# Gated attention in pairs of heads on the two halves of TensorE's array, with the high halves of its result on ScalarE

## What is computed

```python
def gqa_attention(q, k, v):
    B, S, _, HD = q.shape
    G = ATT_HEADS // ATT_KV_HEADS
    nb = S // Q_BLOCK
    qb = q.reshape(B, nb, Q_BLOCK, ATT_KV_HEADS, G, HD).transpose(1, 0, 2, 3, 4, 5)
    scale = HD ** -0.5

    def block(q_blk):
        s = jnp.einsum('bqhgd,bkhd->bhgqk', q_blk, k, preferred_element_type=jnp.float32) * scale
        p = jax.nn.softmax(s, axis=-1).astype(v.dtype)
        return jnp.einsum('bhgqk,bkhd->bqhgd', p, v)
...
        y_att = gqa_attention(q, k, v) @ w_att_out[l]
        y_sgu = spatial_gating(jax.nn.gelu(su), jax.nn.gelu(sv), w_s[l], b_s[l],
                               sgu_ln_g[l], sgu_ln_b[l]) @ w_sgu_out[l]
        merged = jax.nn.sigmoid(ga) * y_att + jax.nn.sigmoid(gb) * y_sgu
        x = x + merged @ w_out[l]
```

## Time and profile before

| | before |
|---|---|
| median of 3 runs (lowest, highest) | 1493.07 us (1492.53, 1499.2) |
| the profiled execution | 1499.87 us |
| its span | 1498.0 us |
| TensorE busy | 1385.2 us (92%) |
| VectorE, ScalarE, GpSimd busy | 616.9, 454.1, 426.5 us |
| mean granted clock of TensorE | 0.975 |
| gated attention, first score to the next stage's first product | 129.41 to 151.84 us |
| chain that ended last | TensorE 66%, DMA 12%, VectorE 10%, GpSimd 5% |

### The profile page before, as it was taken

One profiled execution on the slowest core, in us unless ns is written; L12 is line 12 of the kernel. 1 busy time (PEld: TensorE's weight loads), 2 busy tenths in 40 slices (PEclk: granted clock), 3 DMA queues, 4 the chain that ended last, 5 costly groups with the idle time before them and its releaser, 6 DMA issues.

```text
span 1498.0 us, 22670 instructions
## 1 busy us (share of the span) xinstructions
PE 1385.2 (92%) x8222; PEld 862.5 (58%) x8223; DVE 616.9 (41%) x1323; ACT 454.1 (30%) x786; POOL 426.5 (28%) x197
## 2 busy tenths in 40 slices
PE   7999988899999989997899999899998979999985
PEld 6886776544444488775344444498876844444432
DVE  5598444522122243446233333477015254333324
ACT  4554433212121245543111111245435321112101
POOL 6892743100000077051000000279845610000000
PEclk9999999999999999999999999999998989999998
DMA  7664567699999974419699999795525499999951
GB/s 282 221 191 170 184 225 280 276 426 428 428 429 429 410 282 175 170 57 384 248 384 425 430 428 427 276 342 178 204 78 225 138 376 425 385 427 427 428 202 54
DMA packets 89597, 447.62 MB, mean 299 GB/s; under 512 B 7804, under 2 KB 9768, under 8 KB 70952
## 3 DMA queue, kind: packets, MB, share of 16 engines
q1 hardware_dynamic: 85856, 445.87, 74.8%
q10 hardware_dynamic: 3656, 0.57, 0.3%
HBM read 445.38 MB, written 1.05 MB: 298 GB/s over the span
## 4 chain that ended last, share of the span: by engine, by line
PE 66%; DMA 12%; DVE 10%; POOL 5%; issue 3%; ACT 3%; SPq 0%; DVEq 0%; ACTq 0%; POOLq 0%
PE ps L415 62%; DMA ring_hi<-in_w_up 9%; POOL WLO L2383 4%; PE ps L828 1%; PE ps L868 1%; DMA ring_lo<-in_w_co 1%; ACT WHI L1257 1%; PE ps L849 1%; DVE Z L1846 1%; DVE Z L1834 1%; DVE Z L1847 1%; DVE Z L1845 1%; DMA ring_lo<-in_w_ckv 1%; POOL RS L2352 1%; DMA ring_lo<-in_w_out 1%
## 5 line engine op out<-in xcount | busy, mean ns | idle before, releaser
L2383 POOL TENSOR_TENSOR WLO<-ring_lo,WHI 128x1024 fp32r<-128x1024 f32 (+1 forms) x158 | 386.8, 2470 | 686.5 <-ACT WHI L1257 684.7
L415 PE MATMUL ps<-ring_hi,Z 128*64 128x512 f32 x1248 | 280.1, 598 | 8.1 <-DVE Z L2082 3.0
L415 PE MATMUL ps<-ring_lo,Z 128*64 128x512 f32 x1152 | 261.4, 603 | 6.3 <-issue 5.2
L1257 ACT ACTIVATE WHI<-ring_lo 128x1024 fp32r<-128x1024 f32 (+1 forms) x160 | 165.3, 1048 | 217.5 <-PE ps L415 179.7
L415 PEld LDWEIGHTS ps<-ring_hi,Z 128*64 128x64 f32 x1248 | 90.1, 137 | 175.1 <-issue 168.7
L415 PEld LDWEIGHTS ps<-ring_lo,Z 128*64 128x64 f32 x1152 | 83.1, 139 | 159.6 <-issue 159.1
L2085 DVE TENSOR_TENSOR Z<-ps,Z 64x512 f32<-64x512 f32 x50 | 34.7, 694 | 305.1 <-ACT Z L1446 303.3
L415 PE MATMUL ps<-WHI,HTH 128*128 128x512 f32 x320 | 126.9, 397 | 8.9 <-POOL WLO L2383 5.0
L2352 POOL TENSOR_TENSOR RS<-MS,NEGH 128x1 f32<-128x1 f32 (+2 forms) x26 | 22.3, 857 | 370.2 <-DVE MS L1683 309.7
L1446 ACT ACTIVATE Z<-ps 64x512 f32<-64x512 f32 x50 | 29.5, 590 | 322.1 <-PE ps L415 322.1
L415 PE MATMUL ps<-WHI,HTL 128*128 128x512 f32 x320 | 125.2, 391 | 0.0
(11 more groups left out here) (293 smaller groups left out, 1950.3 us busy)
## 6 DMA issues: line engine op xcount, KB each, us to landing
ring_lo<-in_ada_w SPq DMA_DIRECT2D x22, 2048.0 KB, 9.1
ring_lo<-in_moe_w_gate SPq DMA_DIRECT2D x16, 2048.0 KB, 10.3
ring_lo<-in_moe_w_up SPq DMA_DIRECT2D x16, 2048.0 KB, 14.7
ring_lo<-in_moe_w_down SPq DMA_DIRECT2D x16, 2048.0 KB, 13.8
ring_hi<-in_moe_w_gate SPq DMA_DIRECT2D x16, 2048.0 KB, 11.0
ring_hi<-in_moe_w_up SPq DMA_DIRECT2D x16, 2048.0 KB, 15.5
ring_hi<-in_moe_w_down SPq DMA_DIRECT2D x16, 2048.0 KB, 12.8
ring_lo<-in_ret_w_in SPq DMA_DIRECT2D x12, 2048.0 KB, 8.0
```

Source lines behind the costliest of these rows:

```text
L415: return nc.tensor.matmul(o, l, r, start=start, stop=stop, skip_group_check=True)
L1257: nc.scalar.activation(WHI[:, q, 0:size], slot(r)[:, q * size:(q + 1) * size], Copy).then_inc(S("hi_split"), 1)
L2383: nc.gpsimd.tensor_tensor(WLO[:, q, 0:size], slot(r)[:, q * size:(q + 1) * size], WHI[:, q, 0:size].bitcast(F32), ALU.subtract).then_inc(S ...
```

## The change

The gated attention no longer uses `attention`; each engine has its own loop over four pairs of heads (the cross attention keeps the old function).

- TensorE: `pair_scores(j)` alternates between the heads 2j and 2j+1, first half of the queries for both, then the second. `pair_values(j)` alternates in the same way and waits, before its first product, for the moved probabilities of both heads. Two pairs of scores are made ahead; then per pair: transposes of both heads, pair_scores(j+2), pair_values(j).
- ScalarE: exps(h+2) in place of exps(h+1) stands ahead of the move of head h, and the high halves of the result (`head_high`) are new here, a pair later than the values' own turn.
- VectorE: `values_out` loses the high half; `head_low` makes the low half after it has waited for ScalarE's high half, and stands at the end of a pair.

```diff
+        def pair_scores(j):
+            heads = (2 * j, 2 * j + 1)
+            o = [claim(pe, ("g", "s", h), "B") for h in heads]
+            for t in range(NT):
+                for k, h in enumerate(heads):
+                    ins = mm(o[k][:, t * SEQ:(t + 1) * SEQ], GQT[half_rows(h), j, t * P:(t + 1) * P], GKT[half_rows(h), j // 2, :], t == 0, t == NT - 1)
...
+        def pair_values(j):
+            heads = (2 * j, 2 * j + 1)
+            for h in heads:
+                read(pe, ("g", "p", h))
+            o = [claim(pe, ("g", "v", h), "A") for h in heads]
+            v = slice(64 * (j // 2), 64 * (j // 2) + 64)
+            for c in range(2):
+                for k, h in enumerate(heads):
+                    ins = mm(o[k][half_rows(h), 0:SEQ], GV[:, c, v], probT_buf["g"][h % 2][:, c * SEQ:(c + 1) * SEQ], c == 0, c == 1)
...
+        pair_scores(0)
+        pair_scores(1)
+        ada_panel(0, "A")
+        for j in range(4):
+            head_turn(2 * j)
+            head_turn(2 * j + 1)
+            if j < 2:
+                pair_scores(j + 2)
+            pair_values(j)
...
-        attention("g", 8, ATT_SCALE, {0: 0})
+        def head_exps(h):
+            act.wait_ge(S("g_max"), h + 1)
+            if h >= 2:
+                result(act, ("g", "p", h - 2))
...
+        def head_high(h):
+            o = result(act, ("g", "v", h))
+            r = slice(64 * (h % 2), 64 * (h % 2) + 64)
+            nc.scalar.activation(HTH[r, h // 2, :], o[r, 0:SEQ], Copy).then_inc(S("sv_high"), 1)
+
+        head_exps(0)
+        head_exps(1)
+        ada_copy(0)
+        for j in range(4):
+            for h in (2 * j, 2 * j + 1):
+                if h + 2 < 8:
+                    head_exps(h + 2)
+                if h >= 2:
+                    result(act, ("g", "v", h - 2))
+                move(("g", "p", h), probT_buf["g"][h % 2])
+            if j:
+                head_high(2 * j - 2)
+                head_high(2 * j - 1)
+        head_high(6)
+        head_high(7)
         split_next(("att_out", 0))
...
+        def head_low(h):
+            dve.wait_ge(S("sv_high"), h + 1)
+            o = result(dve, ("g", "v", h))
+            r = half_rows(h)
+            drain(V.tensor_tensor(HTL[r, h // 2, :], o[r, 0:SEQ], HTH[r, h // 2, :].bitcast(F32), ALU.subtract), ("g", "v", h))
+
+        head_maxima(0)
+        head_maxima(1)
+        for j in range(4):
+            for h in (2 * j, 2 * j + 1):
+                head_normal(h)
+                if h + 2 < 8:
+                    head_maxima(h + 2)
+            if j:
+                head_low(2 * j - 2)
+                head_low(2 * j - 1)
+        head_low(6)
+        head_low(7)
```

More of the change, by code:

```diff
@@ L695, in half_rows, with head_turn @@
             return slice(64 * (h % 2), 64 * (h % 2) + 64)
-        attention("g", 8, lambda h: GQT[half_rows(h), h // 2, :], lambda h: GKT[half_rows(h), h // 4, :],
-                  lambda h, c: GV[:, c, 64 * (h // 4):64 * (h // 4) + 64], True, {0: 0})
+        def pair_scores(j):
[4 more added lines that the diff above has]
+                    ins = mm(o[k][:, t * SEQ:(t + 1) * SEQ], GQT[half_rows(h), j, t * P:(t + 1) * P], GKT[half_rows(h), j // 2, :], t == 0, t == NT - 1)
+                    if t == NT - 1:
+                        fill(ins, ("g", "s", h))
+        def head_turn(h):
+            pe.wait_ge(S("g_probs"), h + 1)
+            o = claim(pe, ("g", "p", h), "B")
+            for c in range(2):
+                for t in range(NT):
+                    ins = nc.tensor.transpose(o[:, c * SEQ + t * P:c * SEQ + (t + 1) * P], prob_buf["g"][h % 2][:, t, c * P:(c + 1) * P], ident)
+            fill(ins, ("g", "p", h))
+        def pair_values(j):
[4 more added lines that the diff above has]
+            v = slice(64 * (j // 2), 64 * (j // 2) + 64)
+            for c in range(2):
+                for k, h in enumerate(heads):
+                    ins = mm(o[k][half_rows(h), 0:SEQ], GV[:, c, v], probT_buf["g"][h % 2][:, c * SEQ:(c + 1) * SEQ], c == 0, c == 1)
+                    if c:
+                        fill(ins, ("g", "v", h))
+        pair_scores(0)
[7 more added lines that the diff above has]
+            pair_values(j)
         read(pe, ("ws", 0))
@@ L1389, in attention @@
                 ada_copy(fillers[heads])
-        attention("g", 8, ATT_SCALE, {0: 0})
+        def head_exps(h):
+            act.wait_ge(S("g_max"), h + 1)
+            if h >= 2:
+                result(act, ("g", "p", h - 2))
+            o = result(act, ("g", "s", h))
+            for t in range(NT):
+                ins = nc.scalar.activation(prob_buf["g"][h % 2][:, t, :], o[:, t * SEQ:(t + 1) * SEQ], ACT.Exp,
+                                           bias=SX[:, h % 2, 0, t:t + 1], scale=ATT_SCALE, accum_out=SX[:, h % 2, 1, t:t + 1])
+            drain(ins, ("g", "s", h))
+        def head_high(h):
[17 more added lines that the diff above has]
+        head_high(7)
         split_next(("att_out", 0))
@@ L1905, in half_rows, with head_maxima, head_normal @@
             return slice(64 * (h % 2), 64 * (h % 2) + 64)
-        attention("g", 8, ATT_SCALE, lambda h: (half_rows(h), h // 2))
+        def head_maxima(h):
+            o = result(dve, ("g", "s", h))
+            link(V.tensor_reduce(SX[:, h % 2, 0, :], o.rearrange("p (t k) -> p t k", t=NT), AX, ALU.max))
+            V.tensor_scalar(SX[:, h % 2, 0, :], SX[:, h % 2, 0, :], -ATT_SCALE, None, ALU.mult).then_inc(S("g_max"), 1)
+        def head_normal(h):
+            read(dve, ("g", "s", h))
+            link(V.reciprocal(SX[:, h % 2, 2, :], SX[:, h % 2, 1, :]))
+            for t in range(NT):
+                pr = prob_buf["g"][h % 2][:, t, :]
+                ins = V.tensor_scalar(pr, pr, SX[:, h % 2, 2, t:t + 1], None, ALU.mult)
+            ins.then_inc(S("g_probs"), 1)
+        def head_low(h):
[15 more added lines that the diff above has]
+        head_low(7)
         for t in range(NT):
@@ L2249, in values_out @@
             def values_out(h):
-                dve.wait_ge(S("sv_high"), h + 1)
+                dve.wait_ge(S("sv_high"), 8 + h + 1)
                 o = result(dve, ("sv", h))
```

## The result

| | before | after |
|---|---|---|
| median of 20 runs each (lowest, highest) | 1498.47 us (1492.53, 1504.47) | 1505.49 us (1498.09, 1510.21) |
| after over before, 95% interval | | 1.0043 [1.003, 1.0057] |
| the profiled execution, its span | 1499.87, 1498.0 us | 1501.21, 1499.3 us |
| mean granted clock | 0.975 (profiled execution) | 0.9699 (over the 20 runs) |
| gated attention, first score to next stage's first product | 22.43 us | 27.71 us |

The change costs 0.43%, which is 6.4 us, by its interval 4.5 to 8.5 us (the two medians are 7.0 us apart). That is inside the half per cent, but clear of zero, and more than twice the +3.0 of the forecast. 1505.49 lies 3.0 us above the end of the range, 1502.5. The before kernel itself reads 5.4 us higher over 20 runs than over the three runs shown.

The account below looks back on a forecast made before the run. TensorE was taken to set the pace, VectorE close behind. Queue order +2.0 us and clock +1.0 make +3.0, which on the three runs' median of 1493.07 gives 1496.1 us; range 1488 to 1502.5.

Parts of the forecast that it names:

- The price of a pair: TensorE, gated attention: two heads' products run side by side, 0.95 us for a pair of scores, 1.0 for values.
- The third rival: TensorE: pairs do not run side by side, scores 1.9 us and values 2.0; +7.2 us, 1500.3, chance 0.05.
- The head of the stage: First scores of gated attention: sixteen records in pairs take the same 1.9 us as today's twelve, so nothing is gained.
- The order of the queues: Gated attention: waits between TensorE, ScalarE and VectorE cost +2.0 us, bounds +1.4 and +2.8.
- The walk: Stepping through three engines' queues with expected durations; last values end at 153.9, 2.0 us later than before.
- The new wait of the walk: VectorE: low halves 0 and 1, waiting for ScalarE's high halves, delay head 4's reciprocal from 140.8 to 143.9.
- the cycle: VectorE and ScalarE: each operation of a pair waits for the one before, 6.0 us per two heads instead of 5.3.
- The cover of att_out: After the stage: att_out's later splitting is covered by 0.4 us at first; missing cover may add 0.5 us.
- One more term, the clock: TensorE: sparse work between 144 and 149 lowers the granted clock; +1.0 us taken, between 0 and 1.7.
- The clock rival: TensorE's clock falls and stays low, TensorE halved from 139 on; +14 us, 1507, chance 0.1.
- Throughput of VectorE as the pace: Gated attention: full turns shrink from 2.65 to VectorE's 2.03 us; -4.8 us, 1488.3, chance 0.2.
- The base: Whole kernel: forecast set on the three runs' median, 1493.07 us; the profiled execution, 1499.87, would give 1502.9.

Follow-up runs that it names:

- v2: b1_order with panel product 1 split inside attention, spatial transposes inside att_out, att_out's first quarter split between high halves 5 and 6: ratio to before 0.9994.
- w1_filler: The change plus extra, unread products on TensorE behind each pair's transposes, the values' banks claimed earlier: stage 24.89 us, ratio to before 1.0025.
- c0_change_again: The changed kernel with no edit, run and profiled once more: stage 25.18 us, ratio to before 1.0047.
- w2: The change with only VectorE's low halves moved later, 2 to 7 behind the last normalisation: stage 27.67 us, ratio to before 1.0048.
- f2: The change with both w1_filler's extra products and VectorE's low halves moved late: stage 24.36 us, ratio to before 1.0019.
- b1_order: The change with the queues of TensorE, ScalarE and VectorE all in another order, same work: stage 22.09 us, ratio to before 1.0000.
- b3: b1_order plus two filler products ahead of the scores of heads 4 and 5, the values' banks claimed earlier: stage 20.40 us, ratio to before 0.9999.
- b2: b1_order with both products of one head before both of the other, not alternating: stage 20.36 us, ratio to before 0.9999.

## Why the prediction was wrong, step by step

- **The price of a pair was right.** 0.95 and 1.0 were taken; at full clock a pair of scores takes 1.07 and of values 1.02 (142.94 to 143.96 in v2). The third rival (no running side by side) is out. The head of the stage was taken at 1.9 us and has 1.93 from its first record to the panel product (130.32 to 132.25).
- **The order of the queues was right in kind, half a microsecond short.** The walk put it at +2.0; with the clock held up (w1_filler) it is 24.89 − 22.43 = +2.5. Inside the bounds of +1.4 to +2.8. The transposes of heads 4 and 6 were to be 6.05 us apart; c0_change_again has 6.00 (144.63 to 150.63). The new wait of the walk, "low halves ahead of the next reciprocal", is not all of it: taken away alone it gave 0.0 with the clock down (w2) and 0.5 us with it up (f2), by the estimate there up to 1.2, where the expectation had 1.8. What else closes the cycle stays open. b1_order changes all three queues at once, and no run splits its gain among them.
- **The cover of att_out held.** The splitting was 7.3 us later, not 4.0 (4.8 in c0_change_again), most of it with the stage itself. Yet the load follows the stage's end by 34.8 us in the change as in before, so the half microsecond for the missing cover did not come.
- **"One more term, the clock" is the step that failed.** I took 1.0 of a range of 0 to 1.7. In the profiled execution it is 27.71 − 24.89 = 2.8 us, against 25.18 − 24.89 = 0.3 in the mild one. I had one thin stretch of five microseconds in mind, 144 to 149, and priced one fall from stretches of one length. The change makes gaps from 137 on, and five stretches in a row were granted less than 1.00. Their losses, (0.13 + 0.22 + 0.34 + 0.26 + 0.08) x 5 = 5.2 us of clock, are three times my row's 1.7; about half of it came out as time.
- **The clock rival had the right mechanism and the wrong course**, with a chance of 0.1. It let the clock fall and stay down, to +14. It fell and came back each time, and at 160 was 1.00 again. That 1507 is near to the 1505.49 measured is chance. Between "one stretch" and "to the end" I had no case, and the measured +6.4 lies there.
- **Throughput of VectorE as the pace** (0.2, -4.8): not in this order. In a good order with the clock up the stage falls by 2.0 (b3, b2, v2), not 4.8.
- **The base.** 5.4 us of the miss is the median of three runs that stood below the twenty. The profiled execution (1499.87) and one run of three (1499.2) had said so, and I set the time on the median alone. Of the 9.4 us between 1496.1 and 1505.49, the base is 5.4 and the change 4.0 by the medians (3.4 by the ratio). Set on the twenty runs' median the same +3.0 would have read 1501.5.

Terms together: +2.5 for the order and up to +2.8 for the clock is +5.3 in the profiled stage, and 5.2 at the load. The ratio's +6.4 holds that in its interval (4.5 to 8.5). By ratios the clock is 1.0043 to 1.0025, some 2.7 us with about 3 either way, and the order 3.7 with an interval of 1.3 to 6.1. Both are consistent with the stage, neither is sharper. What stays open is how often the clock falls as in the first profile and how often as in c0, and which property of TensorE's queue decides it: b1 and b2 have the same gaps up to scores 4 and 5 (0.52, 0.86 and 1.29 us), and there one fell to 0.62 between 135 and 140, the other not at all. One thing does go with it, untested: of the eight profiles of changed kernels that have nothing extra in this gap, the three whose first score came before 129.0 us of the span (128.63, 128.69, 128.98) kept 1.00 from 135 to 140, and the five with 129.22 to 130.62 fell to between 0.62 and 0.90.

## What to carry to other kernels

When products are paired, the time saved on TensorE becomes gaps unless ScalarE and VectorE are reordered too: write down for each pair which exponential stands ahead of which move, and walk all queues until they close. Then price the gaps twice, once as waiting and once as clock, over all stretches from the first gap to the end of the stage; here the second was as large as the first in one execution and about a tenth of it in another. A local change of 2 to 5 us in 1500 is read from one stage's stamps and from a later load that carries the shift, not from two spans.

## What the runs showed that I had not expected

- Alternating does not matter; neighbouring in the queue does. Eight records of a pair take 1.07 us in either order.
- With gaps of 0.8 to 2.7 us between work of 1 to 5 us the granted clock fell (0.66 to 0.92 by stretch), and in both profiles with products in those gaps (w1, f2) it was 1.00. The same code falls in one execution and hardly in the next. The Trainium skill (TensorE: Matmul & The Clock Gate, section A second HAM failure mode: psum-queue depth-cycling) tells of another kernel whose clock went up and down because TensorE idled briefly between groups of products; these rows agree in kind.
- A small operation of VectorE from SBUF to SBUF can last as long as GpSimd's beside it. It stands in the trace of before too, at another place, 2.41 us for 128x8 values:

```profile
168.89 2.41 DVE L1793 TENSOR_TENSOR ADA<-ADT,VT 128x8 f32<-128x8 f32 x1
```

with GpSimd's quarter beside it:

```profile
168.88 2.40 POOL L2383 TENSOR_TENSOR WLO<-ring_lo,WHI 128x1024 fp32r<-128x1024 f32 x1 [0.32 <-ACT WHI L1257]
```

VectorE's low halves, which read PSUM, were not held up beside GpSimd (0.44 us each in v2).
